# Attention values computed one step later, directly ahead of the next step's scores, with their output in PSUM bank 7

## The reference

```python
def dilated_attention_mixer(x, positions, k_sh, v_sh, w_q, w_o):
    q = rope((x @ w_q).reshape(B, S, 3 * 16, 64), positions)
    for g, (window, dilation) in enumerate(BRANCHES):      # three branches, 16 heads each
        s = mask(q_g @ k_g.T * 64 ** -0.5)                 # causal, within the window, every dilation-th
        m = max(s); p = exp(s - m); l = sum(p)
        o, lse = p @ v_g / l, m + log(l)
    o = sum over g of softmax(lse over g)[g] * o[g]
    return o.reshape(B, S, 1024) @ w_o
```

## Time and profile before

| | us |
|---|---|
| median of 3 runs | 1110.22 |
| lowest and highest | 1109.82, 1112.21 |
| the profiled execution | 1111.5 |
| its span, first to last instruction | 1109.4 |
| TensorE busy | 1100.3 (99%) |
| VectorE busy | 755.9 (68%) |
| ScalarE busy | 593.4 (53%) |
| granted clock of TensorE | 1.00 throughout |

### The profile page before, as it was taken

One profiled execution on the slowest core, in us unless ns is written; L12 is line 12 of the kernel. 1 busy time (PEld: TensorE's weight loads), 2 busy tenths in 40 slices (PEclk: granted clock), 3 DMA queues, 4 the chain that ended last, 5 costly groups with the idle time before them and its releaser, 6 DMA issues.

```text
span 1109.4 us, 18330 instructions
## 1 busy us (share of the span) xinstructions
PE 1100.3 (99%) x6820; PEld 998.5 (90%) x6820; DVE 755.9 (68%) x1161; ACT 593.4 (53%) x871; POOL 54.5 (5%) x47
## 2 busy tenths in 40 slices
PE   7999999999999999999999999999999999999998
PEld 7998888888999999999988888888999989999987
DVE  6976655564697677676667565655787787989970
ACT  6436654453654655454567454645446756666640
POOL 0100000000000000000000000000110011122210
PEclk9999999999999999999999999999999999999999
DMA  9655756666495454542247657572635564655770
GB/s 279 187 174 169 244 163 204 231 214 203 128 269 152 135 160 124 150 133 76 95 122 221 197 173 238 201 245 71 191 96 181 171 210 134 189 175 184 231 244 19
DMA packets 215670, 193.75 MB, mean 175 GB/s; under 512 B 9609, under 2 KB 190909, under 8 KB 215613
## 3 DMA queue, kind: packets, MB, share of 16 engines
q1 hardware_dynamic: 215401, 192.88, 56.1%
q10 hardware_dynamic: 212, 0.09, 0.0%
HBM read 191.88 MB, written 1.05 MB: 174 GB/s over the span
## 4 chain that ended last, share of the span: by engine, by line
PE 98%; DVE 1%; DMA 1%; ACT 0%; SPq 0%; issue 0%; ACTq 0%
PE ps L665 14%; PE ps L667 14%; PE ps L666 14%; PE ps L610 8%; PE ps L611 8%; PE ps L612 8%; PE ps L764 6%; PE ps L766 6%; PE ps L765 6%; PE ps L819 2%; PE ps L845 2%; PE ps L834 1%; PE ps L853 1%; PE ps L679 1%; PE ps L713 1%; PE ps L677 1%
## 5 line engine op out<-in xcount | busy, mean ns | idle before, releaser
L1648 DVE TENSOR_TENSOR w_lo<-raw,w_hi 128x1024 fp32r<-128x1024 f32 (+1 forms) x298 | 398.9, 1383 | 59.6 <-ACT w_hi L1209 59.2
L1209 ACT ACTIVATE w_hi<-raw 128x1024 fp32r<-128x1024 f32 (+1 forms) x298 | 331.5, 1158 | 121.9 <-PE ps L667 31.6
L610 PE MATMUL ps<-x_hi,w_hi 128*128 128x256 f32 x656 | 186.7, 285 | 0.0
L612 PE MATMUL ps<-x_hi,w_lo 128*128 128x256 f32 x656 | 185.6, 283 | 0.0
L611 PE MATMUL ps<-x_lo,w_hi 128*128 128x256 f32 x656 | 185.6, 283 | 0.0
L665 PE MATMUL ps<-w_hi,x_hi 128*128 128x512 f32 (+1 forms) x328 | 129.4, 394 | 0.0
L667 PE MATMUL ps<-w_hi,x_lo 128*128 128x512 f32 (+1 forms) x328 | 127.5, 389 | 0.0
L666 PE MATMUL ps<-w_lo,x_hi 128*128 128x512 f32 (+1 forms) x328 | 127.3, 388 | 0.0
L610 PEld LDWEIGHTS ps<-x_hi,w_hi 128*128 128x128 f32 x656 | 125.8, 192 | 1.3 <-issue 1.3
L611 PEld LDWEIGHTS ps<-x_lo,w_hi 128*128 128x128 f32 x656 | 125.9, 192 | 0.0
L612 PEld LDWEIGHTS ps<-x_hi,w_lo 128*128 128x128 f32 x656 | 125.8, 192 | 0.0
(11 more groups left out here) (231 smaller groups left out, 1780.0 us busy)
## 6 DMA issues: line engine op xcount, KB each, us to landing
raw<-in_ffn_w_gate_up SPq DMA_DIRECT2D x176, 256.0 KB, 4.1
raw<-in_w_up SPq DMA_DIRECT2D x44, 512.0 KB, 4.4
raw<-in_ffn_w_down SPq DMA_DIRECT2D x24, 768.0 KB, 6.3
raw<-in_conv_w_in SPq DMA_DIRECT2D x24, 512.0 KB, 5.4
raw<-in_w_q SPq DMA_DIRECT2D x48, 256.0 KB, 4.4
raw<-in_w_kv SPq DMA_DIRECT2D x48, 256.0 KB, 4.1
raw_v<-in_w_kv SPq DMA_DIRECT2D x48, 256.0 KB, 4.2
raw<-in_w_in SPq DMA_DIRECT2D x20, 512.0 KB, 4.5
```

The source lines that it names most:

```text
L610: nc.tensor.matmul(o, wh[:, k0 + k, c], hi[:, k, :], start=(k == 0), stop=False)
L612: ins = nc.tensor.matmul(o, wl[:, k0 + k, c], hi[:, k, :], start=False, stop=(k == kt - 1))
L1209: nc.scalar.activation(w_hi[:, s, a * ph.cols:b * ph.cols], src, ACT.Copy)\
L1648: nc.vector.tensor_tensor(w_lo[:, s, c], src, w_hi[:, s, c], ALU.subtract)\
```

## The change

Value is taken out of its place ahead of `turn(2)` and is called at the start of the next step, `value(q - 1)`, with `score` directly behind it; from step 2 on both stand ahead of the first projection tile, and in step 1, which has no value to compute, the scores stay behind the first tile. The tail computes two values. The value output goes to the second half of bank 7 in both query tiles at once (O_AT), so that a matmul of kt = 0 writes 256 columns. The scores move to other banks and get another order, and two waits stand inside them. The copy of the output to y, the storing of the V tiles, and the low and high parts of chunk 2 (the V chunk) change places on ScalarE and VectorE; the first pass of their loops is taken out.

```diff
-        S_AT = ((3 * 512, 5 * 512), (4 * 512, 6 * 512 + 256))
-        S_ORDER = ((0, 0, 0), (1, 1, 0), (0, 0, 1), (0, 0, 2), (1, 0, 0), (0, 1, 0), (1, 0, 1), (1, 0, 2), (0, 1, 1),
-                   (1, 1, 1), (0, 1, 2), (1, 1, 2))
+        S_AT = ((6 * 512, 3 * 512), (6 * 512 + 384, 4 * 512 + 256))
+        S_ORDER = ((0, 0, 0), (1, 1, 0), (0, 0, 1), (0, 0, 2), (1, 1, 1), (0, 1, 0), (1, 1, 2), (0, 1, 1), (1, 0, 0),
+                   (0, 1, 2), (1, 0, 1), (1, 0, 2))
+        O_AT = 7 * 512 + 256
...
@@ TensorE: score
-                    else:
-                        pe.wait_ge(o_stored, q)
                     pe.wait_ge(qk_stored, q * 4 + 4)
...
-                        if (hh, qt, g) == (0, 1, 2):
-                            pe.wait_ge(bank_scored, q + 1)
+                        if (hh, qt, g) == (1, 0, 0):
+                            pe.wait_ge(bank_scored, q * 2 + 2)
+                        if (hh, qt, g) == (1, 0, 1) and not (isinstance(i, int) and i == 1):
+                            pe.wait_ge(o_stored, q)
...
-                        if (hh, qt, g) == (1, 1, 0):
+                        if (hh, qt, g) in ((1, 1, 0), (0, 0, 2)):
                             ins.then_inc(bank_scored, 1)
-                        if (qt, g) == (1, 2):
+                        if (hh, qt, g) in ((0, 1, 2), (1, 0, 2)):
                             ins.then_inc(scored, 1)
@@ TensorE: value
-                        for kt, qt in ((0, 0), (0, 1), (1, 1)):
+                        for kt in range(2):
                             for hh in range(2):
                                 f = slice(hh * HD, (hh + 1) * HD)
...
+                                w = T - kt * P
+                                c = PT_AT[hh][kt] + g * w
+                                ins = nc.tensor.matmul(ps[f, 7, 256 + kt * P:512], v_tok[:, kt, g * P + hh * HD:g * P + (hh + 1) * HD],
+                                                       prob[:, c:c + w], start=(g == 0 and kt == 0), stop=(g == 2 and kt == 1),
+                                                       skip_group_check=True)
@@ TensorE: the step (in the tail, value(q - 1) ahead of score, and value(q) in the old place)
-                    ready(ph, 0, i, bank=False)
-                    pe.wait_ge(qk_stored, 1 if isinstance(i, int) and i == 1 else i * 4)
-                    token_major(ph, 0, 0, banks[0], m_hi, m_lo, signal=1, done=tile_a_done)
-                    score()
+                    if isinstance(i, int) and i == 1:
+                        ready(ph, 0, i, bank=False)
+                        pe.wait_ge(qk_stored, 1)
+                        token_major(ph, 0, 0, banks[0], m_hi, m_lo, signal=1, done=tile_a_done)
+                        score()
+                    else:
+                        value(q - 1)
+                        score()
+                        ready(ph, 0, i, bank=False)
+                        token_major(ph, 0, 0, banks[0], m_hi, m_lo, signal=1, done=tile_a_done)
...
-                    value()
                     turn(2)
@@ ScalarE: store_y, the copy of the output, with act.wait_ge(head_done, q) ahead of it
-                    split(ph, 2, i)
+                    split(ph, 2, i, parts=(0,))
+                    if not (isinstance(i, int) and i == 1):
+                        store_y()
+                    split(ph, 2, i, parts=(1,))
                     exps()
...
@@ ScalarE, tail
                     split(w_o_, 2, 0)
+                    store_y()
                     exps()
+                    act.wait_ge(o_stored, 7)
+                    nc.scalar.activation(m_hi[:, 6, :], y[:, 6, :], ACT.Copy).then_inc(o_hi, 1)
...
@@ VectorE: store_v, now for q; the wait for the values that still read v_tok
-                        dve.wait_ge(tile_a_done, i * 3 + 3)
+                        dve.wait_ge(tile_a_done, q * 3 + 3)
+                        if not (isinstance(i, int) and i == 1):
+                            dve.wait_ge(head_done, q)
...
@@ VectorE, tail
                     split(w_o_, 2, 0, parts=(0,))
+                    store_v(0)
+                    store_v(1)
                     max_of(0)
                     max_of(1)
                     scale(0)
                     scale(1)
+                    output_low(6, 7)
...
@@ VectorE, steps 1 to 7 (store_v and split_next(1) leave the end of step 0)
+                    store_v(0)
+                    store_v(1)
+                    if isinstance(i, int) and i == 1:
+                        split(ph, 1, i)
+                    max_of(0)
+                    max_of(1)
+                    split(ph, 2, i, parts=(0,))
+                    rope(i, 0, banks)
+                    scale(0)
+                    scale(1)
+                    rope(i, 1, banks)
+                    split(ph, 2, i, parts=(1,))
                     split_next(0)
                     rope(i, 2, banks)
                     if last:
                         output_low(0, 6)
                     rope(i, 3, banks)
                     split_next(1)
-                    store_v(0)
-                    if last:
-                        output_low(6, 7)
-                    store_v(1)
```

More of the change, by code:

```diff
@@ L835, in turn_p, with value @@
                     ins.then_inc(prob_turned, 1)
-                def value():
+                def value(q):
                     pe.wait_ge(prob_stored, q + 1)
@@ L1420, in split_next, with store_y @@
                         split(ph, j, i + 1)
+                def store_y():
+                    act.wait_ge(head_done, q)
+                    nc.scalar.activation(y[:, ds(q - 1, 1), :].rearrange("p o t -> p (o t)"), flat[:, O_AT:O_AT + T], ACT.Copy)\
+                        .then_inc(o_stored, 1)
                 if tail:
                     split(w_o_, 2, 0)
+                    store_y()
                     exps()
+                    act.wait_ge(o_stored, 7)
+                    nc.scalar.activation(m_hi[:, 6, :], y[:, 6, :], ACT.Copy).then_inc(o_hi, 1)
                     act.wait_ge(lo_ready, 2 * w_o_.n0)
@@ L1429, in attn_step @@
                     act.wait_ge(head_done, PAIRS)
-                    nc.scalar.activation(m_hi[:, 7, :].rearrange("p (t c) -> p t c", t=2), ps[:, 3:5, 384:512], ACT.Copy)\
-                        .then_inc(o_hi, 1)
+                    nc.scalar.activation(m_hi[:, 7, :], flat[:, O_AT:O_AT + T], ACT.Copy).then_inc(o_hi, 1)
                 elif not attend:
@@ L1543, in emit @@
                     attn_step(0, True, False)
-                    with act.Fori(1, 7) as i:
+                    attn_step(1, True, True)
+                    with act.Fori(2, 7) as i:
                         attn_step(i, True, True)
@@ L1903, in store_v @@
                     if t == 0:
-                        dve.wait_ge(tile_a_done, i * 3 + 3)
-                    else:
-                        dve.wait_ge(product_done, ph.n(3, i) + 1)
-                    nc.vector.tensor_scalar(v_tok[:, t, :], ps[:, banks[4 + t], 0:384], rcol[:, t:t + 1], None, ALU.mult)\
+                        dve.wait_ge(tile_a_done, q * 3 + 3)
+                        if not (isinstance(i, int) and i == 1):
+                            dve.wait_ge(head_done, q)
+                    else:
+                        dve.wait_ge(product_done, ph.n(3, q) + 1)
+                    v_bank = (TILE_BANK_0 if isinstance(i, int) and i == 1 else TILE_BANK)[4 + t]
+                    nc.vector.tensor_scalar(v_tok[:, t, :], ps[:, v_bank, 0:384], rcol[:, t:t + 1], None, ALU.mult)\
                         .then_inc(v_stored if t else va_stored, 1)
@@ L1928, in attn_step @@
                     rope(i, 3, banks)
+                else:
                     store_v(0)
                     store_v(1)
[L1931 to L1934, removed]
+                    if isinstance(i, int) and i == 1:
+                        split(ph, 1, i)
                     max_of(0)
                     max_of(1)
+                    split(ph, 2, i, parts=(0,))
+                    rope(i, 0, banks)
                     scale(0)
+                    scale(1)
                     rope(i, 1, banks)
-                    scale(1)
+                    split(ph, 2, i, parts=(1,))
                     split_next(0)
@@ L2094, in emit @@
                     attn_step(0, True, False)
-                    with dve.Fori(1, 7) as i:
-                        link.enter(i, 8, first=1)
+                    attn_step(1, True, True)
+                    with dve.Fori(2, 7) as i:
+                        link.enter(i, 8, first=2)
                         attn_step(i, True, True)
-                        link.leave(6)
+                        link.leave(5)
                     attn_step(7, True, True, last=True)
```

15 lines of the change are left out of this document (3 added, 12 removed).

## The result

The changed kernel takes 1112.74 us (median of 21 runs, 1111.24 to 1115.62); the kernel before, on the same chip, 1111.46 (21 runs, 1109.73 to 1112.37). The ratio on record is 1.0017 [1.0011, 1.0023], so 1.9 us slower, with an interval of 1.2 to 2.6. The forecast was +1.5 (1111.7 on the scale of 1110.22). The profiled execution took 1112.34, its span is 1110.3.

What follows compares the result with a forecast made beforehand. TensorE, busy 99% of the span, was taken as the bound. Step 1's stall +2.6, moved values -1.0 and wider pieces -.1 gave +1.5 us, so the median of 1110.22 becomes 1111.7; range 1109.1 to 1114.0.

Steps and rivals of the forecast that it cites:

- Step 1: a wait appears: Before turn(0) of step 1, TensorE waits once for VectorE's rope_a: 2.6 us, bounds 2.2 to 2.9.
- Value moved in front of the scores: One array-shape change and one slow load go: .15 us a step, -1.0 over seven; bounds +.3 to -2.4.
- in wider pieces: Value's 18 matmuls become 12 for the same columns: some .01 us a step, -.1 in all.
- in a new order: The new score order starves neither half of the rows: zero, within .05 us a step.
- rival D: Nothing saved at the switch from value to scores, stall as forecast: +2.8 us, 1113.0; chance .12.
- rival C: No stall in step 1, because VectorE gets there sooner: -1.1 us, 1109.1; chance .11.
- Two waits inside the scores: Ninth score matmul waits for the fourth, eleventh for ScalarE's value copy: zero, margins .5 and 1.1 us.
- rival A: The wait for the fourth score matmul bites: .2 us in each of 8 score blocks, +1.6, 1113.3; chance .12.
- VectorE in steps 2 to 7: VectorE's work after the last score takes 7.0 us against 8.6 before turn(0): margin 1.6, zero.
- SyncE's loads: The next V chunk's second half is released some 13 us later; a load takes 4.2 and has 16: zero.
- Tail: Value, scores, then out-projection; its split and store work ends 3.9 us after the last projection, scores 4.4: zero.
- Rival B, the stall lets the clock down: TensorE's clock falls behind step 1's stall: +2 to +4 us, about 1114.7; chance .08.

Runs made afterwards that it cites:

- experiment 6: Changed kernel with step 1's rope(0) ahead of the maxima, plus three projection matmuls moved between value and scores in steps 2 to 7; one execution, 1112.33 us.
- experiment 4: Changed kernel with step 1's rope(0) behind the maxima but ahead of the half split; 1112.15 us, 1.0004 against the kernel before.

## Why the prediction was right, step by step

**Step 1: a wait appears** was right in place, cause and number, with 2.34 for 2.6. VectorE's timeline of the changed kernel, against the earlier trace rows:

```profile
323.71 0.56 DVE L1859 CUSTOM_DVE_ANT_0 prob<-ps,mask 128x384 f32<-128x384 f32 x1 [3.05 <-PE ps L820]
...
326.81 1.75 DVE L1661 TENSOR_TENSOR w_lo<-raw_v,w_hi 128x1536 fp32r<-128x1536 f32 x1
328.48 0.55 DVE L1891 TENSOR_TENSOR rope_a<-ps,cos 128x384 f32<-128x384 f32 x1
...
329.60 0.56 DVE L1894 TENSOR_TENSOR rope_a<-rope_a,rope_b 128x384 f32<-128x384 f32 x1
```

The maxima took 3.1 (323.71 to 326.81), not 3.3: two small clears that stood among them are no longer there in this step, and the split begins before the last small instruction is over; half the split took 1.67, rope(0) 1.68, as laid out; and turn(0) starts .05 after rope_a ends, not .17. The two together are the .3 by which the term was too large (kept to the hundredth, the prediction's own terms give 2.7 and not 2.6). The row that gave .17 was one where TensorE was not waiting at all but busy with value: the distance between an end and the next start is a signal's delay only where the second engine sat idle.

**Value moved in front of the scores, in wider pieces, in a new order**: -.19 a step for -.16, and its parts now have prices of their own. Order .03 (forecast: zero, within .05), wide pieces .03 (.01), and what is left for the switch is .19 - .06 = .13 (.15). Putting a change of shape back between the same blocks cost .20, though between other neighbours than before the change. Either way it lies in the middle of the bounds (-.05 to .35). With it fell rival D, that nothing is saved there, and with the wait of step 1 rival C. What it is made of is in step 4 above: value ends and the scores begin with a pause of .20 from the last start to the first, .09 over the .109 of neighbours, as at the entry from the whole array. So the change from column halves to row halves is one change, not none and not two, as the step assumed. The Trainium skill, "TensorEngine Tiling (Array Packing)", Key Properties, which has a change of mode drain TensorE, agrees with each such pause, though the trace shows the pause and not what fills it. The drains alone, at .09 a change, are some two thirds of the .13 gained and half of the .20 of experiment 6; there the other half is the slow second start.

**Two waits inside the scores**: neither bit, as forecast, and rival A fell. The margins were smaller than said: the ninth score matmul's load starts .26 after the fourth's end (.5 said), the eleventh's .9 after the copy's end (1.1 said). I had taken the start of the matmul; its weights are loaded ahead of it (the eleventh's .11 ahead), and in step 1 the load too stood until rope_a had come: the load of turn(0) starts at 330.21, with the turn itself.

**VectorE in steps 2 to 7, ScalarE, SyncE's loads, Tail**: costed at zero, and no wait appears in any of them. "What is late next is rope(2), and it still has .6" was put to the test by experiment 4 and held to a tenth.

**Rival B, the stall lets the clock down**, had .08 and became true in 10 of 32 executions of the changed kernel, at 1.6 us and not 2 to 4. It was put as all or nothing, with the argument that this stall is half as long as the one that shows it. Neither was so: it happens in some executions and not in others, so it moves the median by little and the upper runs by much. As a mean it is .5 (10/32 x 1.6). This is the term that the sum put at nothing.

**The sum** by measured terms: +2.34 - 1.35 + .5 = +1.5. That this is the forecast to the tenth is luck: the stall came out .3 shorter and the steps' saving .25 larger than said, and the clock's .5, which was not in the sum, made up for both. The two measurements say +1.9 (1.2 to 2.6) and +2.4 (1.4 to 3.4). The first agrees; the second does as well, at its edge. The profiles have nothing above it behind the scores of step 1. The start of the program, which varies by more than that from one execution to the next, is a likely place, but is not shown to be it.

## What to carry to other kernels

Where a loop's first pass has its stages in another order than the rest, check a new order of one engine against that pass by itself: here a stall of 2.3 us in one step of eight undid what the other seven gained, and giving that step its old order back gives the gain back (.9989 on both chips). Before moving work later into a slot ahead of a due time, subtract the idle time that the engine has there, and look at the turn after the one that you have freed: its slack is spent by whatever time you gained. Blocks of matmuls that use the array in different halves are best put side by side, since each return to the whole array between them costs .13 to .20 us.

## What the runs showed of the hardware that I had not expected

Idle time of TensorE of 2.14 to 2.17 us, in a stream that is otherwise dense, was followed by a fall of its clock from 2.4 to 1.2 GHz in 11 of 43 executions; two of .54 and .79 never were in 10, one of 4.29 was in 5 of 5. In the two profiles that show the fall the lower level lasted some 3.4 us, but began at different points: about 1.1 us after the end of the 2.17 (TensorE restarts at 330.21 and slows at 331.3), and in the last tenths of the 4.29 itself. So the wait and what it costs can stand apart in the timeline. It cost 1.6 us in the first and 1.4 in the second. And the order of matmuls on row halves changed what followed them: where one half of the rows ends with its short ones (128 columns), the projection matmuls behind the block start closer together, by .024 us over seven, though both halves stream the same columns in all.
